# Start addresses of the weight buffers and operands in SBUF, rounded to 512 bytes

## The chip, the cores and the metric
The kernel runs on one core of a Trainium2 chip. The metric is the device time of one execution in microseconds. The kernel before takes 3318.09 us, the median of three runs (3317.15 to 3322.59).

## What is computed
Two transformer blocks in a row on 256 tokens of width 2048, all in float32.

```python
h = rmsnorm(x); proj = h @ w_in            # 2048 x 6144, and 8 narrow columns
x = x + concat(stick_breaking(...), forgetting(...)) @ w_out      # 8 + 8 heads of 128
u = relu(rmsnorm(x) @ w_up); x = x + (u * u) @ w_down             # 2048 x 8192 x 2048
x = rmsnorm(x) * g_final
h = x + concat(hgrn2(...), gated_delta(...)) @ w_out_2            # w_in_2: 2048 x 7168 + 16
h = h + peer(rmsnorm(h))                   # 16384 experts, 16 of them for each of 8 heads
return rmsnorm(h) * g_final_2
```

PEER picks experts by two top-16 searches over 128 keys each; the kernel computes it densely: all 16384 hidden values of a token, times a gate that is zero for those not picked, times all of v.

## The kernel before
**Weights.** Every large weight matrix comes in chunks of 128 partitions x 2048 float32 values (1 MB), by one DMA each, into one of four slots of `raw`. ScalarE copies a slot into `hi` as fp32r (L255), VectorE subtracts, raw - hi, into `lo` or, where `lo`'s place is in use for other data, into `lo_in`, which lies over `raw` (L262). The activations are split in the same way: `xh` and `xl`, `coef_h` and `coef_l`, `cV_h` and `cV_l`. TensorE then computes three products for each piece: high x high, high x low and low x high. A slot is free again when TensorE has used it (`pe_used`).

**Two shapes of product.** In `multiply` (L273 to L275), and in the dense parts of the two blocks (L818 to L820, L1637 to L1639), 128 x 128 of an activation is the stationary operand (the weights that TensorE loads) and 512 columns of the weight buffer move. A chunk takes 24 such matmuls. In `multiply_up` (L287 to L289) 128 columns of the weight buffer are stationary and the 256 tokens of `xh` or `xl` move; a chunk takes 48. The MLP has 64 chunks of each kind, PEER's down products 128. In a row of the trace the moving operand is named first, the stationary one last.

```python
nc.tensor.matmul(pair[:, t, :], sh[:, k0 + k, tok], hi[:, j, cols], start=begin, stop=False)
nc.tensor.matmul(o, hi[:, j, cols], xh[:, k0 + k, :], start=clears, stop=False, skip_group_check=True)
```

**Stages in time.** Block 1 with its attentions until 443 us; the MLP until about 1140 us, in which up (L287 to L289) and down products (L273 to L275 with coef) alternate; block 2 until 1744 us; the router's query and PEER's up products until 2587 us (L287 to L289); PEER's down products (L273 to L275 with cV) until 3303 us; then the last norm and the output. From 2063 us on, groups of four small gate products (L2118, `hotG` moving and `hotA` stationary) stand between the up products, 64 groups in all. L478 are transposes; L536 and L538 are the narrow products for the 8 or 16 columns beyond the large matrix, whose stationary operand is `wtail_s[:, k, ...]`, 128 bytes further on for each k; L1027 and L1028 are decay sums, with both operands in `split2`.

**Where tensors lie.** A cursor gives out addresses in each partition, rounded up to 32 bytes (L127 to L136). The program's base is 1121, so `raw` begins at 1152. `region(at)` (L163) places tensors one behind another from a given address: `at_lo` for what lies over `lo` during the two blocks, `at_y` for what follows `xl`. The positions in bytes, and past a multiple of 512:

| Tensors | Address | Past 512 |
|---|---|---|
| raw, lo_in | 1152 | 128 |
| hi | 33920 | 128 |
| lo, and the tensors laid over it | 66688 | 128 |
| resid, cst, small | 99456, 115840, 126080 | 128 |
| wtail_s | 128192 | 192 |
| xh, xl | 131392, 147776 | 320 |
| proj1, proj2, split2, hid, coef_h, coef_l, hotA, hotG, cV_h, cV_l, hidV, gateV | from 164160 | 320 |

The slices that large products read begin at multiples of 512 bytes within these tensors. The last tensor ends at 228480; 229368 is the end of what is usable.

**Order of the work.** Each engine has its own program, written out by hand in the order of the chunks; loops run over pairs of blocks in the MLP and in PEER's down products. Nothing in it depends on addresses.

Of the kernel before, what the change touches and what calls it, by code (L numbers as in the profile page):

```python
# [116 lines left out]
def two_blocks(nc, x_d, xT_d, cst_d, att_d, small_d, gfin1_d, gfin2_d, wf_d, wba_d, keys_d,  # L117
# [5 lines left out]
    with ctx:  # L123
        def sem(name):
            return ctx.enter_context(nc.semaphore(name))

        cursor = [(nc.sbuf_base + 31) // 32 * 32]  # L127

        def sb(name, shape, dt=F32, at=None):

            size = 4 * int(np.prod(shape[1:]))
            t = nc.alloc_sbuf_tensor_at(name, shape, dt, offset=cursor[0] if at is None else at)
            if at is None:
                cursor[0] += (size + 31) // 32 * 32
            return t
# [19 lines left out]
        tail = sb("tail", [P, TT, 16])  # L155
        tail_t = sb("tail_t", [32, TT * P])

        at_x = cursor[0]
        xh = sb("xh", [P, KT, TT * P], F32R)
        xl = sb("xl", [P, KT, TT * P], F32R)  # L160
# [2468 lines left out]
```

How the kernel before makes its waits and increments, by code:

```python
        def link(eng, s, n, ins):  # L240
            n[0] += 1
            ins.then_inc(s, 1)
            eng.wait_ge(s, n[0])
# [6 lines left out]
        def make_hi(act, q, j, first=False):  # L251
            act.wait_ge(raw_ready[j], q * 16 + 16)
            if not first:
                act.wait_ge(pe_used, q * SLOTS + j - 3)
            nc.scalar.activation(hi[:, j, :], raw[:, j, :], ACT.Copy).then_inc(hi_ready, 1)
# [4 lines left out]
        def make_lo(dve, q, j):  # L260
            dve.wait_ge(hi_ready, q * SLOTS + j + 1)
            nc.vector.tensor_tensor(low(q)[:, j, :], raw[:, j, :], hi[:, j, :].bitcast(F32),
                                    ALU.subtract).then_inc(lo_ready, 1)
# [1 line left out]
        def multiply(pe, q, j, pair, sh, sl, k0, first, last):  # L265
            pe.wait_ge(lo_ready, q * SLOTS + j + 1)
            for k in range(4):
                cols = slice(k * NB, (k + 1) * NB)
                for t in range(TT):
                    tok = slice(t * P, (t + 1) * P)
                    begin, end = first and k == 0, last and k == 3
                    nc.tensor.matmul(pair[:, t, :], sh[:, k0 + k, tok], hi[:, j, cols], start=begin, stop=False)
                    nc.tensor.matmul(pair[:, t, :], sh[:, k0 + k, tok], lo[:, j, cols], start=False, stop=False)
                    mm = nc.tensor.matmul(pair[:, t, :], sl[:, k0 + k, tok], hi[:, j, cols], start=False, stop=end)
            mm.then_inc(pe_used, 1)
# [139 lines left out]
        def spread_dve(dve, n, wide):  # L416
            dve.wait_ge(nm_rs, n + 1)
            for t in range(TT):
```

## Time and profile before

| | |
|---|---|
| Median of three runs | 3318.09 us |
| Span of the profiled execution | 3316.7 us |
| PE busy | 3251.2 us, 98% |
| PEld (weight loads, beside the matmuls) | 2896.3 us, 87% |
| DVE busy | 2039.7 us, 61% |
| ACT busy | 1459.5 us, 44% |
| POOL busy | 486.7 us, 15% |
| DMA | 194 GB/s over the span |

The span runs from the first to the last instruction of the profiled execution. Matmuls are pipelined: one is shown with its whole length, and the next begins before it ends, so that the distance from start to start is its cost and not its length. A busy PE isn't PE at its peak. Engine names in the rows: PE is TensorE, PEld its weight loads, DVE VectorE, ACT ScalarE, POOL GpSimd.

### The profile page before, as it was taken

How to read it: one execution, taken by the hardware profiler on the slowest of the kernel's cores; microseconds unless marked ns; L12 is line 12 of the kernel's file. 1: busy time of each engine (PE TensorE's matmuls, PEld its weight loads, DVE VectorE, ACT ScalarE, POOL GpSimd, SP SyncE). 2: the span in 40 equal slices, each digit the busy share in tenths (PEclk: the TensorE clock that was granted, in tenths of full speed). 3: DMA queues.
4: the chain of work that ended last, by engine and by line, in shares of the span. 5: the costliest groups of instructions: out<-in, count | busy, mean ns of one | idle time of the engine just before them, and what ended most of it. 6: DMA issues, size and time to landing. Idle time of an engine off the chain costs nothing.

```text
span 3316.7 us, 48331 instructions
## 1 busy us (share of the span) xinstructions
PE 3251.2 (98%) x20054; PEld 2896.3 (87%) x20054; DVE 2039.7 (61%) x1849; ACT 1459.5 (44%) x1268; POOL 486.7 (15%) x418
## 2 busy tenths in 40 slices
PE   7999999999999989999999999999999999999998
PEld 6788899999999878888879999999999888888886
DVE  4455565555555557665456888999874555455554
ACT  5564453344333464453334444455543333333333
POOL 0000000000000002135200002888840000000000
PEclk9999999999999999999999999999999999999999
DMA  6444465555555443342245565676676666556563
GB/s 255 141 164 165 154 229 191 191 191 194 193 193 190 141 164 127 130 150 89 90 164 217 194 223 216 213 247 234 230 252 239 231 236 251 221 224 253 231 237 114
DMA packets 131396, 644.18 MB, mean 194 GB/s; under 512 B 14640, under 2 KB 47664, under 8 KB 61872
## 3 DMA queue, kind: packets, MB, share of 16 engines
q1 hardware_dynamic: 96016, 624.18, 52.4%
q10 hardware_dynamic: 35232, 17.83, 1.8%
q8 instruction: 116, 1.90, 0.2%
q14 instruction: 32, 0.26, 0.0%
HBM read 606.31 MB, written 35.66 MB: 194 GB/s over the span
## 4 chain that ended last, share of the span: by engine, by line
PE 92%; DVE 3%; ACT 2%; DMA 1%; issue 1%; SPq 0%; DVEq 0%; ACTq 0%
PE pj L288 12%; PE pj L289 12%; PE pj L287 12%; PE pj L275 7%; PE pj L274 7%; PE pj L273 7%; PE pj L1637 3%; PE pj L1639 3%; PE pj L1638 3%; PE pj L818 3%; PE pj L820 3%; PE pj L819 3%; PE pm L273 2%; PE pt L273 2%; PE pt L274 2%; PE pm L275 2%
## 5 line engine op out<-in xcount | busy, mean ns | idle before, releaser
L255 ACT ACTIVATE hi<-raw 128x2048 fp32r<-128x2048 f32 x535 | 1025.0, 1916 | 1419.2 <-PE pj L289 661.5
L262 DVE TENSOR_TENSOR lo<-raw,hi 128x2048 fp32r<-128x2048 f32 x400 | 917.1, 2293 | 714.3 <-ACT hi L255 713.7
L287 PE MATMUL pj<-xh,hi 128*128 128x256 f32 x3328 | 927.0, 279 | 0.0
L289 PE MATMUL pj<-xh,lo 128*128 128x256 f32 x3328 | 926.1, 278 | 0.0
L288 PE MATMUL pj<-xl,hi 128*128 128x256 f32 x3328 | 926.0, 278 | 0.0
L287 PEld LDWEIGHTS pj<-xh,hi 128*128 128x128 f32 x3328 | 630.8, 190 | 0.6
L288 PEld LDWEIGHTS pj<-xl,hi 128*128 128x128 f32 x3328 | 625.0, 188 | 0.6
L289 PEld LDWEIGHTS pj<-xh,lo 128*128 128x128 f32 x3328 | 624.8, 188 | 0.0
L262 DVE TENSOR_TENSOR lo_in<-raw,hi 128x2048 fp32r<-128x2048 f32 x135 | 311.4, 2310 | 281.3 <-ACT hi L255 280.7
L2314 POOL TENSOR_SCALAR hotA<-cst,slotT 128x128 fp32r<-128x128 f32 x256 | 328.2, 1297 | 496.2 <-ACT slotT L2157 435.8
L1637 PE MATMUL pj<-hi,xh 128*128 128x512 f32 x576 | 235.7, 409 | 13.4 <-ACT proj L1706 7.3
L1639 PE MATMUL pj<-hi,xl 128*128 128x512 f32 x576 | 229.0, 398 | 0.0
L818 PE MATMUL pj<-hi,xh 128*128 128x512 f32 x512 | 211.0, 412 | 18.3 <-DVE lo_in L2481 11.9
L1638 PE MATMUL pj<-lo_in,xh 128*128 128x512 f32 x576 | 227.4, 395 | 0.0
L274 PE MATMUL pj<-lo,cV_h 128*128 128x512 f32 x512 | 203.5, 397 | 0.0
L275 PE MATMUL pj<-hi,cV_l 128*128 128x512 f32 x512 | 203.5, 397 | 0.0
L273 PE MATMUL pj<-hi,cV_h 128*128 128x512 f32 x512 | 203.5, 397 | 0.0
L820 PE MATMUL pj<-hi,xl 128*128 128x512 f32 x512 | 203.5, 397 | 0.0
L819 PE MATMUL pj<-lo_in,xh 128*128 128x512 f32 x512 | 202.6, 396 | 0.0
L275 PE MATMUL pj<-hi,coef_l 128*128 128x512 f32 x512 | 201.7, 394 | 0.0
L274 PE MATMUL pj<-lo,coef_h 128*128 128x512 f32 x512 | 200.6, 392 | 0.0
L273 PE MATMUL pj<-hi,coef_h 128*128 128x512 f32 x512 | 199.0, 389 | 0.0
(382 smaller groups left out, 4269.8 us busy)
## 6 DMA issues: line engine op xcount, KB each, us to landing
raw<-w_peer SPq DMA_DIRECT2D x256, 1024.0 KB, 6.1
raw<-w_mlp SPq DMA_DIRECT2D x128, 1024.0 KB, 4.9
raw<-w_in SPq DMA_DIRECT2D x104, 1024.0 KB, 4.9
raw<-w_out SPq DMA_DIRECT2D x32, 1024.0 KB, 4.8
raw<-w_q SPq DMA_DIRECT2D x16, 1024.0 KB, 5.0
act_scratch<-hidU SPq DMA_DIRECT2D x32, 512.0 KB, 3.1
gates_scratch<-stage ACTq DMA_DIRECT2D x8, 2048.0 KB, 16.9
hidV<-act_scratch SPq DMA_DIRECT2D x32, 512.0 KB, 3.7
```

The source lines that it names most:

```text
L255: nc.scalar.activation(hi[:, j, :], raw[:, j, :], ACT.Copy).then_inc(hi_ready, 1)
L262: nc.vector.tensor_tensor(low(q)[:, j, :], raw[:, j, :], hi[:, j, :].bitcast(F32), ALU.subtract).then_inc(lo_ready, 1)
L273: nc.tensor.matmul(pair[:, t, :], sh[:, k0 + k, tok], hi[:, j, cols], start=begin, stop=False)
L274: nc.tensor.matmul(pair[:, t, :], sh[:, k0 + k, tok], lo[:, j, cols], start=False, stop=False)
L275: mm = nc.tensor.matmul(pair[:, t, :], sl[:, k0 + k, tok], hi[:, j, cols], start=False, stop=end)
L287: nc.tensor.matmul(o, hi[:, j, cols], xh[:, k0 + k, :], start=clears, stop=False, skip_group_check=True)
L288: nc.tensor.matmul(o, hi[:, j, cols], xl[:, k0 + k, :], start=False, stop=False, skip_group_check=True)
L289: mm = nc.tensor.matmul(o, lo[:, j, cols], xh[:, k0 + k, :], start=False, stop=end and b % 2 == 1, skip_group_check=True)
L1637: nc.tensor.matmul(pair[:, t, :], xh[:, k0 + kk, tok], hi[:, j, cols], start=begin, stop=False)
L1638: nc.tensor.matmul(pair[:, t, :], xh[:, k0 + kk, tok], lo_in[:, j, cols], start=False, stop=False)
L1639: mm = nc.tensor.matmul(pair[:, t, :], xl[:, k0 + kk, tok], hi[:, j, cols], start=False, stop=end)
L2314: ins = nc.gpsimd.tensor_scalar(hotA[u % 2][:, a, :], cst[:, C_IOTA, :], slotT[:, 0, tok:tok + 1], None, ALU.is_equal)
```

## The change
The first address is rounded up to 512 bytes instead of 32, and the cursor is rounded up to 512 once more ahead of `xh`. All that is placed relative to them moves along. The roundings of 32 between tensors stay.

```diff
-        cursor = [(nc.sbuf_base + 31) // 32 * 32]
+        cursor = [(nc.sbuf_base + 511) // 512 * 512]
...
         tail = sb("tail", [P, TT, 16])
         tail_t = sb("tail_t", [32, TT * P])
 
+        cursor[0] = (cursor[0] + 511) // 512 * 512
         at_x = cursor[0]
         xh = sb("xh", [P, KT, TT * P], F32R)
         xl = sb("xl", [P, KT, TT * P], F32R)
```

## Rows read from the trace of the kernel before

**Rows 1.** The page: busy time by engine, and the chain that ended last.
```profile
PE 3251.2 (98%) x20054; PEld 2896.3 (87%) x20054; DVE 2039.7 (61%) x1849; ACT 1459.5 (44%) x1268; POOL 486.7 (15%) x418
...
PE 92%; DVE 3%; ACT 2%; DMA 1%; issue 1%; SPq 0%; DVEq 0%; ACTq 0%
```
**Rows 2.** Costliest groups: line, tiles, shapes, count | busy us, mean ns | idle before.
```profile
L287 PE MATMUL pj<-xh,hi 128*128 128x256 f32 x3328 | 927.0, 279 | 0.0
...
L1637 PE MATMUL pj<-hi,xh 128*128 128x512 f32 x576 | 235.7, 409 | 13.4 <-ACT proj L1706 7.3 <-DVE resid L1844 3.6 <-DVE xl L493 2.5
...
L818 PE MATMUL pj<-hi,xh 128*128 128x512 f32 x512 | 211.0, 412 | 18.3 <-DVE lo_in L2481 11.9 <-DVE lo_in L262 5.1 <-ACT proj L867 1.3
```
**Rows 3.** TensorE by stretches: from:to us, length, busy (matmuls), clock, DMA share, GB/s.
```profile
1860.00:2040.00 180.00, 180.00 (x1591) 1.00 0.60 217
2485.00:2585.00 100.00, 100.00 (x852) 1.00 0.63 232
2600.00:3300.00 700.00, 700.00 (x3001) 1.00 0.58 223
```
**Rows 4.** In order of time, MLP down products: start us, length us, line.
```profile
532.97 0.39 PE L275 MATMUL pj<-hi,coef_l 128*128 128x512 f32 x1
...
534.34 0.39 PE L275 MATMUL pj<-hi,coef_l 128*128 128x512 f32 x1
```
**Rows 5.** In order of time, first gate groups of PEER.
```profile
2063.28 0.28 PE L287 MATMUL pj<-xh,hi 128*128 128x256 f32 x1
...
2063.62 0.28 PE L287 MATMUL pj<-xh,hi 128*128 128x256 f32 x1
...
2064.43 0.28 PE L287 MATMUL pj<-xh,hi 128*128 128x256 f32 x1
...
2069.26 0.28 PE L289 MATMUL pj<-xh,lo 128*128 128x256 f32 x1
...
2069.97 0.28 PE L289 MATMUL pj<-xh,lo 128*128 128x256 f32 x1
2070.09 0.64 PE L2118 MATMUL pt<-hotG,hotA 128*128 128x256 f32 x4
2070.57 0.28 PE L287 MATMUL pj<-xh,hi 128*128 128x256 f32 x1
```
**Rows 6.** In order of time, block 1 while the clock is at half.
```profile
13.28 0.63 PE L818 MATMUL pj<-hi,xh 128*128 128x512 f32 x1
13.71 0.63 PE L819 MATMUL pj<-lo_in,xh 128*128 128x512 f32 x1
```
**Rows 7.** Groups of ScalarE and VectorE, 2600 to 3300 us.
```profile
L255 ACT ACTIVATE hi<-raw 128x2048 fp32r<-128x2048 f32 x122 | 233.8, 1917 | 421.0 <-PE pj L275 221.9 <-PE pm L275 114.2 <-PE pt L275 84.9
...
L262 DVE TENSOR_TENSOR lo<-raw,hi 128x2048 fp32r<-128x2048 f32 x123 | 282.0, 2293 | 333.7 <-ACT hi L255 333.7
```
**Rows 8.** In order of time, the two series of narrow products.
```profile
61.01 0.28 PE L536 MATMUL pm<-xh,wtail_s 128*16 128x256 f32 x1
...
61.94 0.28 PE L536 MATMUL pm<-xh,wtail_s 128*16 128x256 f32 x1
...
1194.97 0.28 PE L538 MATMUL pm<-xl,wtail_s 128*16 128x256 f32 x1
...
1195.87 0.28 PE L538 MATMUL pm<-xl,wtail_s 128*16 128x256 f32 x1
```
**Rows 9.** In order of time, a group of decay sums and the products before it.
```profile
1245.74 0.39 PE L1637 MATMUL pj<-hi,xh 128*128 128x512 f32 x1
...
1246.43 0.40 PE L1027 MATMUL pj<-split 128*128 128x512 f32 x1
...
1247.36 0.39 PE L1637 MATMUL pj<-hi,xh 128*128 128x512 f32 x1
```
**Rows 10.** L287 alone by stretches.
```profile
2063.00:2587.00 524.00, 392.00 (x1395) 1.00 0.68 235
```
## The prediction, made before the change was run

> **What bounds the kernel now.** I read the page's shares first: TensorE's matmuls are busy 98% of the 3316.7 us and hold 92% of the chain that ended last [rows 1]. So only two things can move the time: the holes between matmuls, and the pace at which matmuls follow one another. The holes are small. The costliest groups of matmuls show idle time only at their first lines, 18.3 us at L818 and 13.4 us at L1637 [rows 2], and the clock is granted in full nearly everywhere [rows 3]. What is left is the pace.
>
> The list in order of time and the table by stretches give the pace, since the start of one matmul to the start of the next is what each costs (the 279 to 412 ns of one matmul overlap its neighbours [rows 2]). In the down products of the MLP, starts of L275 lie at 532.97 and, six matmuls later, at 534.34: 1.37 us for six matmuls of 512 columns, 228.3 ns each [rows 4]. In the last stage 3001 matmuls of 512 columns fill 700.00 us: 233.3 ns [rows 3]. The up products, 256 moving columns each, take 180.00/1591 = 113.1 ns before the gate products begin at 2063 us and 100.00/852 = 117.4 ns after them [rows 3]. The tensors and positions are the same in both stretches of up products. The pace changes between 2063.84 and 2064.43 us, when the first four L2118 matmuls pass (three steps take 0.34 us from 2063.28 to 2063.62 and 0.35 to 0.36 us after it), and is still slow in the stretch of rows 3 after the last of them [rows 3, 5].
>
> How much of this is overhead? At the lower clock, in the first microseconds, 512 columns take 13.71 - 13.28 = 0.43 us, which is 512 columns at 1.2 GHz and nothing else [rows 6]. At 2.4 GHz the columns alone take 213.3 ns and 106.7 ns, so 15 to 20 ns and 6 to 11 ns per matmul come on top. There are 3 x 3328 = 9984 matmuls of 256 columns and 3 x (576 + 512) = 3264 of 512 in the blocks (one of three lines each in [rows 2]), and by the chunks 64 x 24 = 1536 in the MLP and 128 x 24 = 3072 in the last stage, 7872 of 512 together. One nanosecond of pace is 18 us.
>
> **What the change does, part by part.** It adds and removes no instruction, DMA or wait. It moves every buffer from raw on by 384 bytes, and xh, xl and all that lies behind them by another 320. In bytes past a multiple of 512, raw, hi, lo, resid, cst and the tensors laid over lo go from 128 to 0; xh, xl, proj1, proj2, coefficients and gate tensors go from 320 to 0. All slices of them that the large products read start at multiples of 512 bytes within the tensor, so today a weight slice and its partner are always 192 bytes apart (modulo 512), and afterwards 0. The small tensors between, wtail_s among them, stay off 512.
>
> DMA, ScalarE and VectorE: at work beside TensorE. In the last stage the hi copies keep ScalarE busy 233.8 us and the lo subtractions VectorE 282.0 us of 700 [rows 7]. A cost of some per cent on them is covered: the 421.0 and 333.7 us for which they idle before those lines are waits for TensorE's release of a slot and for each other. I take 0; without that cover it would be 123 x 2293 ns x the share by which they slow down, some 3 us a per cent in this stage. Buffers still fit; no other tile moves relative to its region.
>
> TensorE is therefore the whole sum, and no row of this kernel shows an operand at 0. Three readings bound it.
>
> First, the step from 256 to 512 columns costs 233.3 - 117.4 = 115.9 ns in the slow pace and 228.3 - 113.1 = 115.2 ns in the fast one, against 106.7 ns for 256 columns at 2.4 GHz [rows 3, 4]. So 1024 further bytes cost 8.5 to 9.2 ns extra, 4.3 to 4.6 ns per 512. And the two paces of one and the same product differ by 117.4 - 113.1 = 4.3 ns, or 233.3 - 228.3 = 5.0 ns: again one such piece. A moving operand of 1024 bytes that starts at 128 or 320 touches three pieces of 512 where an aligned one touches two; of 2048 bytes, five instead of four. I read the slow pace as the one in which that further piece is paid, and the fast one as that in which it is hidden.
>
> Second, the narrow products at L536 and L538 read weights at 192, 320, 448 and 64 in turn, so their distance from the moving operand changes from step to step. In the first series, at 61 us, eight of them take 61.94 - 61.01 = 0.93 us, 116 ns each; in the second, at 1195 us, eight take 1195.87 - 1194.97 = 0.90 us, 113 ns [rows 8]. So position seems to count in the slow condition and not in the fast one.
>
> Third, pairs that are already 0 apart (both at 320) are slower than their neighbours. From the L289 before a group of four L2118 to the L287 behind it are five steps, four of them into weights 0 apart: 2070.57 - 2069.97 = 0.60 us, 120 ns each, where the six before take 0.71 us, 118 ns [rows 5]. The four products L1027/L1028 of 512 columns run from 1246.43 to 1247.36 us, 232.5 ns each, where the three before them take 0.69 us, 230 ns [rows 9]. This speaks for a cost of equal positions and against the change.
>
> Bounds per matmul, then: -4.3 ns on every one, also those now fast; +4.2 ns on 512 columns (232.5 - 228.3) and, for 256 columns, up to the 120 ns of the L2118 groups, +6.9 ns on those at the quick pace. **The value I take** is -4.3 ns for the slow up products and -5.0 ns for the slow down products, nothing for those that are fast. It is nearest to what this kernel shows of itself with the same instructions:
> - up products after 2063 us: 3 lines x 1395 = 4185 [rows 10], x 4.3 ns = 18.0 us
> - down products of the last stage: 3072, x 5.0 ns = 15.4 us
> - all others (5799 up, 4800 of 512 columns): 0
> Sum -33.4 us. The profiled execution spans 3316.7 us, 1.4 us under the median of 3318.09 us; so 3283.3 in its own time, 3285 us as the median. Nothing is late next: TensorE stays busy to the end, and what follows its last product is a chain of norm and output that doesn't change.
>
> The Trainium skill would cap the gain. Its page "TensorE: Matmul & The Clock Gate", section "Back-to-back issue gap", gives N/2.4 + 2.5 ns for isolated matmuls, 215.8 and 109.2 ns for these widths. By it, an estimate for a kernel freed of all overhead is 12.5 to 17.5 ns less on 7872 products and 4 to 8 ns less on 9984, some 170 us. The rows never show such a pace for these products.
>
> **Rivals.**
> *Nothing moves.* Both old positions are already multiples of 64 bytes; if only that counts, or if the two paces come from how the stream restarts after a wait, the time is 3318 us. For it: the pace of L287 to L289 changed with the first L2118 group and all their positions unchanged [rows 5], and the second series of L536 is indifferent to position [rows 8]. Against it: the first series. A rule of the Trainium skill says the same by another road: the page "SBUF — State Buffer", section "Who interferes with whom", gives TensorE two independent read ports, for moving data and for weights, and says that it waits on no one; by that rule equal positions can't collide and I would forecast 3318. Its section "Operand start alignment" asks only for the element's size and says that it is about legality, not speed. The first series of rows 8 disagrees or at least isn't explained by it.
>
> *Equal positions collide.* The next weights are read while a matmul streams (weight loads are busy 87% of the span beside the matmuls' 98% [rows 1]); 0 apart, both reads can begin in the same piece each time. Price: 5799 fast up products x 6.9 ns (120 - 113.1) = 40 us, 4185 at the slow pace x 2.6 ns = 11 us, 4800 of 512 columns x 4.2 ns = 20 us, the last stage at its 233.3 already: +71 us, 3389 us. If only the fast condition is lost and nothing beyond, it is 5799 x 4.3 + 4800 x 5.0 = +49 us, 3367 us. It decides the sign as soon as more than some 33 us of this is paid on top of my gain. For it: the L2118 groups and L1027/L1028 [rows 5, 9]. Against it: all of those stand at 320, so that they can't tell equal positions from a start off 512, and in the second series of rows 8 one step in four is 0 apart and costs nothing.
>
> *All go one piece down.* The fast products also lose 4.3 ns: another 10599 x 4.3 = 46 us, 3239 us. No row shows such a pace.
>
> **How the numbers follow.** My forecast, 3285 us, 0.35; one piece down for all or most, near 3239 us, 0.10; nothing, 3318 us, 0.20; collision, 3350 (half of it) to 3389 us, 0.35. Two tenths of a per cent (6.6 us) is about what a measurement of this kernel can tell from no change. Faster 0.45, same 0.20, slower 0.35. The likeliest's own range is 3270 to 3305 us. The range for 8 in 10 runs from 3234 to 3388 us: both unknown signs are in it, and each end leaves about a tenth out.
>
> **What would show it.** In the profile after, the up products of 1860 to 2040 us and of 2485 to 2585 us should have one pace, 113 ns, and the last stage 228 to 229 ns. If 512-byte pieces don't matter, the same two paces at the same places remain. Had equal positions collided, up products in the MLP would stand at 117 to 120 ns and the down products at 232 ns or more. L262 and L255 should keep 2293 and 1917 ns. The forecast is wrong if the MLP's paces move up, or if the last stage stays at 233.3 ns.

## The result

The changed kernel takes 3336.09 us (median of 4 runs, 3334.73 to 3339.56) beside 3320.34 us for the kernel before in the same runs: a ratio of 1.005, 95% interval 1.0038 to 1.0063. It is slower by half a per cent, where 3285 us and a gain of 1% were forecast. The profiled execution spans 3334.7 us, 18.0 us more than before.

**The profile after.** All line numbers behind L157 are one higher. First the page, in the same order as [rows 1]: busy time, the chain that ended last, then VectorE's lo subtraction and the matmul groups of [rows 2], with busy us, mean ns | idle us before.

```profile
PE 3267.7 (98%) x20054; PEld 2936.5 (88%) x20054; DVE 2039.2 (61%) x1849; ACT 1459.1 (44%) x1268; POOL 482.6 (14%) x418
...
PE 92%; DVE 3%; ACT 2%; issue 1%; SPq 1%; DMA 1%; DVEq 0%; ACTq 0%
...
L263 DVE TENSOR_TENSOR lo<-raw,hi 128x2048 fp32r<-128x2048 f32 x400 | 916.7, 2292 | 737.0 <-ACT hi L256 735.7
L288 PE MATMUL pj<-xh,hi 128*128 128x256 f32 x3328 | 942.6, 283 | 0.0
...
L1638 PE MATMUL pj<-hi,xh 128*128 128x512 f32 x576 | 233.6, 406 | 13.7 <-ACT proj L1707 7.4
L819 PE MATMUL pj<-hi,xh 128*128 128x512 f32 x512 | 208.9, 408 | 19.3 <-DVE lo_in L2482 13.1
```

TensorE alone has changed, as supposed: VectorE and ScalarE are as busy as before (2039.2 and 1459.1 us against 2039.7 and 1459.5), the lo subtraction takes 2292 ns against 2293, and the idle times before the block lines hardly move. One matmul of the up products has grown, 283 ns for 279; those of the blocks have shrunk, 408 and 406 for 412 and 409.

The pace by stretches, which answers to [rows 3] (from:to us, length, busy us with the number of matmuls, clock, DMA share, GB/s):

```profile
1860.00:2040.00 180.00, 180.00 (x1503) 1.00 0.56 202
2515.00:2615.00 100.00, 100.00 (x836) 1.00 0.64 237
2640.00:3310.00 670.00, 670.00 (x2958) 1.00 0.60 233
```

And in order of time (start us, length us), the MLP's down products, as in [rows 4], and the first gate group, as in [rows 5]:

```profile
533.24 0.39 PE L276 MATMUL pj<-hi,coef_l 128*128 128x512 f32 x1
...
534.60 0.39 PE L276 MATMUL pj<-hi,coef_l 128*128 128x512 f32 x1
...
2092.61 0.28 PE L288 MATMUL pj<-xh,hi 128*128 128x256 f32 x1
...
2093.21 0.28 PE L290 MATMUL pj<-xh,lo 128*128 128x256 f32 x1
2093.33 0.64 PE L2119 MATMUL pm<-hotG,hotA 128*128 128x256 f32 x4
2093.81 0.28 PE L288 MATMUL pj<-xh,hi 128*128 128x256 f32 x1
```

Up products now step evenly by 0.12 us: 2092.61 to 2093.21 is 0.60 us for five, 120 ns, and so are the five from 2093.21 to 2093.81 across the gate group. Nothing changes at the gate groups any more. The down products take 1.36 us for six, 226.7 ns, in the MLP and 670/2958 = 226.5 ns in the last stage. So two paces for each width have become one for each: 120.0 ns for 256 columns, slower than both of before, and 226.7 ns for 512 columns, quicker than both. (A stretch counts the matmuls that reach over its ends too, so its quotient is up to 0.4 ns lower than the steady pace; the table goes by starts.) The quick pace of the down products before, which I had read as 228.3 ns from starts six apart, is 228.9 ns over 95 steps:

```profile
488.07 0.39 PE L273 MATMUL pj<-hi,coef_h 128*128 128x512 f32 x1
...
509.81 0.39 PE L275 MATMUL pj<-hi,coef_l 128*128 128x512 f32 x1
```

| Products | Number | Before, ns | After, ns | us |
|---|---|---|---|---|
| up, before the gate groups | 5799 | 113.3 | 120.0 | +38.9 |
| up, from the gate groups on | 4185 | 117.8 | 120.0 | +9.2 |
| down, MLP | 1536 | 228.9 | 226.7 | -3.4 |
| down, last stage | 3072 | 233.3 | 226.7 | -20.3 |
| the two blocks | 3264 | 228.9 | 226.7 | -7.2 |

That is +17.2 us beside a span that grew by 18.0 us. The blocks' pace is taken from their steady parts.

### The profile page after: what moved, and what is told of

Its sections match the earlier page's. It is cut to its first block, busy times and chain, and to the rows that moved or that the text cites. A ratio compares the mean times of both kernels' runs of the same rounds, so it can differ in the third digit from the quotient of the medians.

```text
span 3334.7 us, 48331 instructions
## 1 busy us (share of the span) xinstructions
PE 3267.7 (98%) x20054; PEld 2936.5 (88%) x20054; DVE 2039.2 (61%) x1849; ACT 1459.1 (44%) x1268; POOL 482.6 (14%) x418
## 4 chain that ended last, share of the span: by engine, by line
PE 92%; DVE 3%; ACT 2%; issue 1%; SPq 1%; DMA 1%; DVEq 0%; ACTq 0%
PE pj L289 12%; PE pj L290 12%; PE pj L288 12%; PE pj L274 7%; PE pj L275 7%; PE pj L276 7%; PE pj L1638 3%; PE pj L1640 3%; PE pj L1639 3%; PE pj L819 3%; PE pj L821 3%; PE pj L820 3%; PE pt L274 2%; PE pt L276 2%; PE pm L274 2%; PE pm L276 2%
## 5 line engine op out<-in xcount | busy, mean ns | idle before, releaser
L263 DVE TENSOR_TENSOR lo<-raw,hi 128x2048 fp32r<-128x2048 f32 x400 | 916.7, 2292 | 737.0 <-ACT hi L256 735.7
L288 PE MATMUL pj<-xh,hi 128*128 128x256 f32 x3328 | 942.6, 283 | 0.0
L290 PE MATMUL pj<-xh,lo 128*128 128x256 f32 x3328 | 941.8, 283 | 0.0
L289 PE MATMUL pj<-xl,hi 128*128 128x256 f32 x3328 | 941.8, 283 | 0.0
L289 PEld LDWEIGHTS pj<-xl,hi 128*128 128x128 f32 x3328 | 638.9, 192 | 0.5
L288 PEld LDWEIGHTS pj<-xh,hi 128*128 128x128 f32 x3328 | 638.8, 192 | 0.6
L290 PEld LDWEIGHTS pj<-xh,lo 128*128 128x128 f32 x3328 | 638.8, 192 | 0.0
L1639 PE MATMUL pj<-lo_in,xh 128*128 128x512 f32 x576 | 226.7, 394 | 0.0
```

The costliest lines, as they stand in the source:

```text
L263: nc.vector.tensor_tensor(low(q)[:, j, :], raw[:, j, :], hi[:, j, :].bitcast(F32), ALU.subtract).then_inc(lo_ready, 1)
L289: nc.tensor.matmul(o, hi[:, j, cols], xl[:, k0 + k, :], start=False, stop=False, skip_group_check=True)
L290: mm = nc.tensor.matmul(o, lo[:, j, cols], xh[:, k0 + k, :], start=False, stop=end and b % 2 == 1, skip_group_check=True)
L1639: nc.tensor.matmul(pair[:, t, :], xh[:, k0 + kk, tok], lo_in[:, j, cols], start=False, stop=False)
```

## The experiments

Two theories came first. **R**: what counts is the distance between the moving operand and the weights that are loaded while it moves, modulo some number. **S**: what counts is whether an operand starts at a multiple of 512, which is what my forecast rested on. In what follows, "distance" is the moving operand's position less that of the stationary one.

### One part of the change alone, and the same distance off 512

half1 has the first rounding only, half2 the second only:

```diff
-        cursor = [(nc.sbuf_base + 31) // 32 * 32]
+        cursor = [(nc.sbuf_base - 0 + 511) // 512 * 512 + 0]
```

```diff
+        cursor[0] = (cursor[0] - 0 + 511) // 512 * 512 + 0
         at_x = cursor[0]
```

equal_off leaves `raw` at 128 past 512 and puts `xh` at 128 too; opposite has `raw` at 0 and `xh` at 256:

```diff
+        cursor[0] = (cursor[0] - 128 + 511) // 512 * 512 + 128
         at_x = cursor[0]
```

Expected of half1: 

> Only the first rounding: raw, hi, lo start at 0 past a multiple of 512, xh and all behind it at 192. The distance between weight buffer and activation operand stays 192, as in the kernel before. Theory R (the distance of the two operands modulo 512 sets the pace): the paces of before come back, up products 113 to 118 ns, down products 229 to 233 ns, 3318 us within 5 us. Theory S (a start at a multiple of 512 sets the pace): the down products, whose moving operand hi is now at 0, run at 226.7 ns as in the changed kernel, while the up products, whose moving operand xh is at 192, stay at 113 to 118 ns; that would be some 30 us less than before, 3288 us.

Expected of half2: 

> Only the second rounding: hi and lo stay at 128, xh and all behind it go to 0; the distance is 384. R: new paces at both widths, different from those at 192 and at 0; not known in size, between 113 and 120 ns and between 224 and 234 ns. S: the up products, whose moving operand is at 0, run at 120.0 ns as in the changed kernel, the down products at 229 to 233 ns as before: some 47 us more than before, 3365 us.

Expected of equal_off: 

> Weight buffers and activation operands all start at 128 past a multiple of 512: distance 0, no start on 512. R: the changed kernel's paces, 120.0 ns and 226.7 ns at every stage, 3336 us within 5 us. S: the paces of before, 113 to 118 and 229 to 233 ns, 3318 us.

Expected of opposite: 

> Weight buffers at 0, activation operands at 256: half of 512 apart. R: paces of its own; if the cost is a collision of the two reads near their starts, this is the farthest from it and up products run at 113.3 ns throughout, the down products at 227 to 229 ns, 3270 to 3290 us. S: down products 226.7 ns, up products 113 to 118 ns, 3288 us; up products at 120 ns here would speak against both.

Measured, against 3320.97 us of the kernel before on the same chip: half1 3318.28 us (ratio 0.9995, 0.9985 to 1.0005), half2 3366.60 us (1.0137, 1.0120 to 1.0154), equal_off 3338.02 us (1.0060, 1.0043 to 1.0077), opposite 3337.94 us (1.0055, 1.0038 to 1.0072). Their stretches, one fence for each kernel in this order; the second line lies in the last up products, the third in the last stage:

```profile
1860.00:2040.00 180.00, 180.00 (x1591) 1.00 0.61 217
2500.00:2580.00 80.00, 80.00 (x681) 1.00 0.64 237
2660.00:3300.00 640.00, 640.00 (x2745) 1.00 0.57 221
```
```profile
1860.00:2040.00 180.00, 180.00 (x1504) 1.00 0.55 197
2500.00:2580.00 80.00, 80.00 (x677) 1.00 0.69 244
2660.00:3300.00 640.00, 640.00 (x2756) 1.00 0.61 236
```
```profile
1860.00:2040.00 180.00, 180.00 (x1504) 1.00 0.57 202
2500.00:2580.00 80.00, 80.00 (x669) 1.00 0.69 250
2660.00:3300.00 640.00, 640.00 (x2826) 1.00 0.61 236
```
```profile
1860.00:2040.00 180.00, 180.00 (x1504) 1.00 0.56 202
2500.00:2580.00 80.00, 80.00 (x670) 1.00 0.69 250
2660.00:3300.00 640.00, 640.00 (x2825) 1.00 0.61 236
```

Three things show here. half1, in which hi and lo stand at 0, has the paces of before to the count (1591 matmuls in 180 us, as in [rows 3]; 640/2745 = 233.2 ns): a start at 512 is worth nothing by itself, and theory S falls. equal_off, in which nothing starts at 512, has those of the changed kernel (119.7 and 640/2826 = 226.5 ns). And opposite, 256 apart, can't be told from 0 apart, at either width: so I count distances modulo 256 and not 512. My guess that 256 would be the farthest from a collision was wrong for that reason. half2, 128 apart, is the slowest kernel so far, since it is near the slow end at both widths, 119.7 and 232.2 ns: the second part of the change alone costs 1.4%, the first nothing, and both together 0.5%. S had forecast half2's time, 3365 us, almost to the point; with half1 and equal_off against it, that was luck. R had given no more than a range of paces there.

### Other distances

The same edit with `xh` at 192, 352, 288 and 160 past 512, `raw` at 128:

```diff
+        cursor[0] = (cursor[0] - 192 + 511) // 512 * 512 + 192
         at_x = cursor[0]
```

Expected of d64: 

> Weight buffers at 128, activation operands at 192. The earlier four kernels show equal paces wherever the distance is equal modulo 256. Here an up product's moving operand lies 64 bytes ahead of the weights being loaded (192 in the kernel before) and a down product's 192 ahead (64 before). If only the size of the gap to the nearest multiple of 256 counts, not its sign, all paces are those of before, 3318 us. If the sign counts, up and down products change places in what they lose: up products slower than 113 to 118 ns, down products other than 229 to 233 ns.

Expected of off224: 

> Weight buffers at 128, activation operands at 352: 224 ahead for up products, 32 for down products. If the reads go in pieces of 64 bytes, a start in the middle of one costs a further piece: up products over 113.3 ns by 7 ns or more. If only the distance counts and runs on smoothly, up products lie between 113.3 (distance 192) and 120.0 ns (distance 0), down products between 226.7 and 233.3 ns.

Expected of off160: 

> Activation operands at 288: distance 160 for up products, 96 for down products, between 192/64 (113.3 to 117.7, 228.9 to 233.3 ns) and 128/128 (118.7, 232.3 ns). If whole pieces of 64 bytes count, a start in the middle of one costs as at 224: up products about 118.3 ns, down products 233.3 ns, 3362 us. If the cost runs smoothly with the distance, up products 113.3 to 118.7 ns, down 229 to 233 ns, about 3340 us.

Expected of off32: 

> Activation operands at 160: 32 ahead of the weights for up products, 224 for down products; the mirror image of off224. By pieces of 64 bytes, about 118 and 233 ns again, 3360 us; if near-equality with 0 counted, 120 and 227 ns, 3336 us.

Measured: d64 3348.90 us (3339.05 to 3363.08; ratio 1.0096, 1.0063 to 1.0129), and in one run each off224 3364.84, off160 3364.80, off32 3350.73 us. The stretches of d64:

```profile
1860.00:2040.00 180.00, 180.00 (x1532) 1.00 0.57 201
2500.00:2580.00 80.00, 80.00 (x708) 1.00 0.64 234
2660.00:3300.00 640.00, 640.00 (x2744) 1.00 0.59 229
```

d64 turns the picture round. Its up products run at 117.5 ns first and at 80/708 = 113.0 ns in the late stretch, and its down products at 233.2 ns. So 256 columns have the same two paces, 113.3 and 117.8 ns, at 64 and at 192, while for 512 columns the two distances differ. All seven distances, ns per matmul from the same stretches:

| Kernel | Up: distance mod 256 | Up, early / late | Down: distance | Last stage |
|---|---|---|---|---|
| after, equal_off, opposite | 0 | 119.7 / 119.6 | 0 | 226.5 |
| off32 | 32 | 116.5 / 116.3 | 224 | 233.2 |
| d64 | 64 | 117.5 / 113.0 | 192 | 233.2 |
| half2 | 128 | 119.7 / 118.2 | 128 | 232.2 |
| off160 | 160 | 118.3 / 118.2 | 96 | 233.2 |
| before, half1 | 192 | 113.1 / 117.5 | 64 | 233.2 |
| off224 | 224 | 118.0 / 117.8 | 32 | 233.2 |

off160 came out as expected of whole pieces of 64 bytes (118.3 and 233.3 ns, 3362 us). But the same idea wanted 7 ns or more on off224's up products, where 5 were measured, and the up products of off32, at 116.5 ns, miss both numbers that I had given for them; its down products have the 233 ns of one. So that idea doesn't hold as it stands. Steps of 32 bytes bring nothing: within this list the best place for up products is 64 or 192, for down products 0. One address rule for both can't be the best.

### Only the down products' operands, only the gate operands

coef_equal moves the operands of the down products, so that they are 0 apart from the weight buffers, and leaves xh. What is placed behind them in the same region moves by 64 bytes too, rs_wide among it:

```diff
+        y("pad_c", [P, 16])
         coef_h = [y(f"coef_h{i}", [P, 4, TT * P], F32R) for i in range(2)]
...
+        y("pad_v", [P, 16])
         cV_h = [y(f"cV_h{i}", [P, 4, TT * P], F32R) for i in range(2)]
```

hot_apart moves only the operands of the gate products to a distance of 192 modulo 256, as the up products have it; hot1, which no matmul reads, goes elsewhere to make room:

```diff
-        hot1 = y("hot1", [P, 4, NK])
+        hot1 = region(at_z)("hot1", [P, 4, NK])
+        y("pad_a", [P, 16])
         hotA = [y(f"hotA{i}", [P, 4, NK], F32R) for i in range(2)]
+        y("pad_g", [P, 48])
         hotG = [y(f"hotG{i}", [P, 4, 2, NK], F32R) for i in range(2)]
```

Expected of coef_equal: 

> Only coef_h, coef_l, cV_h and cV_l are moved, by 64 bytes, so that they and the weight buffers are 0 apart modulo 256; xh and xl stay where they were. If the distance modulo 256 of each pair sets its pace, the MLP's down products go from 228.9 to 226.7-227.0 ns, the last stage from 233.3 to 226.7 ns, and the up products keep 113.3 and 117.7 ns: 20.4 + 2.9 = 23 us less than before, 3295 us. If the pace hangs on something else in where xh lies, nothing changes.

Expected of hot_apart: 

> Only the gate products' operands move: hotA (stationary) to 128 and hotG (moving) to 320 past a multiple of 512, so that at L2118 the moving operand is 192 ahead modulo 256 of every weight load next to it, as in the up products; hot1 is put elsewhere to make room. If the first group of them, which were 0 apart, throws TensorE out of the 113.3 ns pace and it doesn't come back by itself, the up products after 2063 us now keep 113.3 ns and the last stage runs at 228.9 ns: 18 + 14 = 32 us less than before, 3286 us. If the change of pace has another cause (GpSimd's work from 2063 us on, or the restart after a wait), 3318 us and the same 117.7 and 233.3 ns.

coef_equal: 3306.28 us against 3320.89 (0.9959, 0.9945 to 0.9974). The last stage did what was expected (first fence, by stretches: 226.5 ns), but the total gains 15 us and not 23, mainly because up products of the MLP now stand at the pace of 118 ns, 0.71 us for six (second fence, in order of time), though none of their operands moved:

```profile
2600.00:3260.00 660.00, 660.00 (x2914) 1.00 0.62 239
```
```profile
509.99 0.28 PE L288 MATMUL pj<-xh,hi 128*128 128x256 f32 x1
...
510.70 0.28 PE L288 MATMUL pj<-xh,hi 128*128 128x256 f32 x1
```

The trace shows where that began: not at the down products, the first of which comes at 487.86 us, but at four small products (L426; L425 in the kernel before) at 470.45 us that turn rs_wide into a row. Nine steps before them take 1.02 us, 113 ns each, and nine after them 1.06 us, 118 ns (first fence). In the kernel before, the same nine after them take 1.02 us (second fence, beginning behind the four). By their positions, cst and rs_wide are 0 apart modulo 256 in coef_equal, since rs_wide moved by 64, and 64 apart before. (best, further down, has no pad ahead of coef_h and keeps 113 ns in the MLP.)

```profile
469.32 0.28 PE L290 MATMUL pj<-xh,lo 128*128 128x256 f32 x1
...
470.34 0.28 PE L290 MATMUL pj<-xh,lo 128*128 128x256 f32 x1
470.45 0.60 PE L426 MATMUL pm<-cst,rs_wide 128*128 128x128 f32 x4
...
471.13 0.28 PE L290 MATMUL pj<-xh,lo 128*128 128x256 f32 x1
...
472.19 0.28 PE L290 MATMUL pj<-xh,lo 128*128 128x256 f32 x1
```
```profile
471.97 0.28 PE L289 MATMUL pj<-xh,lo 128*128 128x256 f32 x1
...
472.99 0.28 PE L289 MATMUL pj<-xh,lo 128*128 128x256 f32 x1
```

hot_apart: 3285.71 us (0.9890, 0.9874 to 0.9907), and 3286 us was expected; its profiled execution spans 31.2 us less than that of before. Its stretches, the last up products and the last stage, and its gate group in order of time:

```profile
2460.00:2560.00 100.00, 100.00 (x885) 1.00 0.68 249
2600.00:3260.00 660.00, 660.00 (x2885) 1.00 0.59 229
```
```profile
2072.50 0.28 PE L289 MATMUL pj<-xh,lo 128*128 128x256 f32 x1
2072.62 0.62 PE L2120 MATMUL pt<-hotG,hotA 128*128 128x256 f32 x4
2073.07 0.28 PE L287 MATMUL pj<-xh,hi 128*128 128x256 f32 x1
```

From L289 to L287 across the four gate products it is 0.57 us, 114 ns a step, where it was 0.60 us in [rows 5]. The up products keep 100/885 = 113.0 ns to their end, and the last stage runs at 660/2885 = 228.8 ns. So 256 small matmuls, 30 us of work, had held 7257 others in the slower of two paces. A third theory, **M**, follows: at a distance of 64 or 192 the stream of up products has two steady paces; a few products at distance 0 can throw it from one to the other, and it stays where it lands.

### A control, and the best of both

hot_control keeps all of hot_apart except the second pad, so that hotG is 0 apart from hotA again. best is hot_apart with `pad_v` of coef_equal, but without `pad_c`.

```diff
-        y("pad_g", [P, 48])
```

Expected of hot_control: 

> Control for hot_apart: hot1 is put elsewhere and hotA moved by the same 64 bytes, but hotG, hotA's partner, follows directly and is 0 apart from it again. If the distance at L2118 made the difference in hot_apart, the up products fall to 117.7 ns from 2063 us on and the last stage to 233.3 ns, 3318 us. If hot1's place or the shift of the other tensors did it, 113.3 and 228.9 ns remain, 3286 us.

Expected of best: 

> The gate operands 192 apart as in hot_apart, and cV_h, cV_l 0 apart from the weight buffers as in coef_equal, but coef_h and coef_l of the MLP left where they were, since the MLP's up products lost 4 ns when they were moved. Up products after 2063 us 113.3 ns, last stage 226.7 ns instead of 228.9: 3285.7 - 3071 x 2.2 ns = 3279 us, 1.2% under the kernel before. If moving cV changes the up products ahead of it too, 18 us more, 3297 us.

hot_control: 3296.04 us (two runs; 0.9923, 0.9903 to 0.9942), between the two numbers expected. In order of time, around its second gate group:

```profile
2068.83 0.28 PE L289 MATMUL pj<-xh,lo 128*128 128x256 f32 x1
...
2070.25 0.28 PE L289 MATMUL pj<-xh,lo 128*128 128x256 f32 x1
2070.36 0.64 PE L2119 MATMUL pt<-hotG,hotA 128*128 128x256 f32 x4
...
2071.20 0.28 PE L287 MATMUL pj<-xh,hi 128*128 128x256 f32 x1
...
2072.10 0.28 PE L289 MATMUL pj<-xh,lo 128*128 128x256 f32 x1
```

Before the group 12 steps take 1.42 us, 118 ns; after it 8 steps take 0.90 us, 113 ns. Each group turns the pace over, to slow and back, and the last of 64 leaves it at the quick one, so that the last stage has hot_apart's 228.8 ns. The two kernels differ in nothing that TensorE reads but the place of hotG. So it is shown that the place of the gate operands turns the pace, and that the pace then stays.

Which way it turns, and whether it does, hotG's distance to hotA alone does not settle. In the kernel before, the first group turns the pace to slow and the other 63 leave it there. In d64, where hotG and hotA are 0 apart too, the pace was already quick when the first group came at 2103.11 us, and all 64 groups leave it so. It had changed at 2091.57 us, at six products that turn `res` (L2108): nine steps before them take 1.06 us, nine after them 1.02 us.

```profile
2090.39 0.28 PE L290 MATMUL pj<-xh,lo 128*128 128x256 f32 x1
...
2091.45 0.28 PE L290 MATMUL pj<-xh,lo 128*128 128x256 f32 x1
2091.57 0.82 PE L2108 MATMUL pm<-cst,res 128*128 128x128 f32 x6
...
2092.45 0.28 PE L290 MATMUL pj<-xh,lo 128*128 128x256 f32 x1
...
2093.47 0.28 PE L290 MATMUL pj<-xh,lo 128*128 128x256 f32 x1
```

best: 3281.54 us against 3321.63 us for the kernel before (ratio 0.9875, 0.9859 to 0.9892); 3279 us was expected. In the times alone, its lead on hot_apart is within the spread of the runs. It beats the kernel before and the changed one, with up products at 113.1 ns and the last stage at 660/2913 = 226.6 ns, where hot_apart has 228.8:

```profile
2460.00:2560.00 100.00, 100.00 (x884) 1.00 0.69 257
2600.00:3260.00 660.00, 660.00 (x2913) 1.00 0.60 231
```

## Why the prediction was wrong

**What bounds the kernel**: right. Only the pace of matmuls moved, and ScalarE, VectorE and DMA stayed covered.

**The first reading of three is the step that failed.** I took the slow pace as one in which "that further piece is paid", a piece of 512 bytes that an aligned operand doesn't touch, so that the change would take it away. The sum had worked out twice, 4.3 to 4.6 ns per 512 bytes from the widths and 4.3 to 5.0 ns between the two paces, and I took the agreement for evidence. half1 and equal_off show that a start at 512 counts for nothing. The price per width isn't one of length either: at distance 0 both widths carry the same 13.3 ns on top of their columns (120.0 - 106.7 and 226.7 - 213.3). What stands in place of that step is the distance between the two operands: the change took it from 192 to 0 for the up products, which cost 48 us, and from 64 to 0 for the down products and the blocks, which gave 31 us back.

**Terms of the sum.** Slow up products, -4.3 ns forecast: +2.2 ns measured. Up products at the quick pace, 0 forecast: +6.7 ns, the 38.9 us that decide the sign. Last stage, -5.0 ns forecast: -6.6 ns; right in direction by luck, since the cause is another. Down products of the MLP and products of the blocks, 0 forecast: -2.2 ns. The measured time lies in the range for 8 in 10, 3234 to 3388 us, but no theory of the prediction gives it: it falls between "nothing", 3318, and half a collision, 3350.

**The rival of equal positions** named the right place and had the up products' price: 120 ns, from the L2118 groups of [rows 5], and 51 us of cost; measured 48 us. It was wrong on 512 columns. The 232.5 ns of L1027/L1028 [rows 9] were four matmuls among others at another distance, and I read them as the steady pace at distance 0. In the changed kernel, where their neighbours are 0 apart too, the same four take 0.91 us (1261.00 to 1261.91 us), some 227 ns each. That reading put +20 us on the products of the MLP and the blocks and 0 on the last stage, where -31 us came out. That is why it stood at 3389 us and not at 3336. It also counted "both reads can begin in the same piece each time" as a cost at every width, where distance 0 is the worst for 256 columns and the best for 512. And in [rows 8], counted modulo 256, two steps in four are 0 apart and not one; the second series still takes 113 ns a step, so that these narrow products, with 16 stationary columns, don't follow the wide ones.

**Why the pace changed at 2063 us** was left as a riddle, and it held the larger part of the gain that best has. The hint stood in [rows 5]: the change came with four matmuls whose operands lie otherwise to each other than all others around. I had listed it as evidence that nothing moves.

**The rule on ports.** The Trainium skill, page "SBUF — State Buffer", section "Who interferes with whom", gives TensorE independent read ports for moving data and weights, and says that it waits on no one. The runs disagree as far as timing goes: with everything else equal, the place of one operand against the other moves the pace of up products from 113.1 to 119.7 ns and that of down products from 226.5 to 233.2 ns. Whether it is the two reads that meet, or something else that depends on both addresses, no run here shows.

Left open: why 64 and 192 have two paces; what decides whether a few other products turn them; why the down products prefer 0 and the up products don't; and why the four timed runs of d64 spread over 24 us (3339.05 to 3363.08). A late stage that stays at 117.8 ns in some executions would be, by an estimate, 4185 x 4.5 ns = 19 us of it, but only the run of 3339.05 us has a trace.

## What to carry to other kernels

When TensorE is over 95% busy, measure the distance from start to start of matmuls in steady stretches, and compare it with columns / 2.4 GHz: 6.6 to 20 ns stood here on top of each fp32r product in steady stretches, and up to 6.7 ns of that hung on where the operands lie to each other modulo 256 bytes, not on round starts. Choose that distance for each kind of product by itself, and try it, since one rounding for all gave half a per cent away and three pads gained 1.2%. A pace that changes for good at one place in a program, with the same instructions before and after, points at what stands at that place. And a pad moves all that is placed behind it: in coef_equal it was a small tensor behind the pad, not the padded ones, that cost the MLP its quick pace.

## What the runs showed of the hardware

- At distance 0 modulo 256 a 128-column weight load with an fp32r matmul of 256 columns repeats every 120.0 ns, of 512 columns every 226.7 ns: 13.3 ns over the columns in both cases.
- At 64 or 192 the 256-column product has two steady paces, 113.3 and 117.8 ns; at 64 the 512-column product has 228.9 and 233.3 ns, and at 192 it was seen at 233.2 ns alone. The pace in force can outlast hundreds of microseconds, and was seen to change at a few other matmuls: four gate products (the kernel before, 2063.96 us), four that turn rs_wide (coef_equal, 470.45 us), six that turn res (d64, 2091.57 us).
- The distance counts modulo 256 as far as was tried: 256 (opposite) gave 180/1504 us and 640/2825 us where 0 (equal_off) gave 180/1504 and 640/2826. No other two distances 256 apart were compared.
